# Spreading a slot's small TensorE jobs over the quarters of the next chunk, in a two-layer decoder step

## The reference

```python
# layer 0
z = rms_norm(h, pre_g) @ w_in              # 2048 x 6144: u, pool gate, q, k, v, attention gate
pool_out = pool_linear(window_means(u) - u) * pool_scale      # windows 2, 4, 8, 16
q, k = partial_rope(q), partial_rope(k)    # 8 heads, two 64-wide maps each
o = (softmax(q1 k1) - lam * softmax(q2 k2)) @ v               # causal; sample rows read a paged cache
mix = [pool_out * silu(pool_gate), rms_norm(o) * 0.8 * silu(attn_gate)]
h = h + rms_norm(mix @ w_out, post_g)
# layer 1
z = rms_norm(h, pre_g) @ w_in              # 2048 x 6160: q, k, v, gate, low rank
g = log_sigmoid(lr @ wa2 + ba) / 16
o, state = gla_scan(q, k, v, g, state)     # 4 heads, gated linear attention, causal
h = h + rms_norm((rms_norm(o) * silu(gate)) @ w_out, post_g)
```

## Time and profile before

| | |
|---|---|
| runs | 2369.33, 2361.41, 2366.83 us; median 2366.83 |
| span of the profiled execution | 2367.4 us, and no time of its own beside it |
| TensorE, DVE, ACT, POOL busy | 91%, 35%, 27%, 34% of the span |
| mean granted TensorE clock | 0.924 of 2.4 GHz |
| where the time lies | start to 60 us, four pairs to 1047, output projection to 1248, layer 1's norm to 1307, four heads to about 2133, output projection to 2327, results to the end |

### The profile page before, as it was taken

The page is one execution under the profiler, slowest core; times in us unless marked ns, Lnnn a source line. Parts: engine busy times, 40 slices in busy tenths (PEclk is TensorE's granted clock), DMA queues, the critical chain, the costliest instruction groups (busy, mean ns, idle before and its releaser), DMA issues.

```text
span 2367.4 us, 40345 instructions
## 1 busy us (share of the span) xinstructions
PE 2160.6 (91%) x15341; PEld 1989.5 (84%) x15341; DVE 827.4 (35%) x1391; ACT 646.5 (27%) x1158; POOL 816.3 (34%) x369
## 2 busy tenths in 40 slices
PE   6987998799979997889997999999999999979996
PEld 5986897698869887779995997898799789859995
DVE  4345224522444234550007225305423430642004
ACT  5121212212221212132214324323332332432222
POOL 2242233312241324245546332241232134225554
PEclk8997899879988899789998999999999999989997
DMA  6433333332343234343322354244334424434332
GB/s 209 129 103 90 92 100 86 107 90 75 97 125 93 69 87 116 97 139 97 88 74 97 85 145 143 73 117 134 118 91 132 143 74 124 126 106 145 89 89 73
DMA packets 357441, 252.57 MB, mean 107 GB/s; under 512 B 15135, under 2 KB 324784, under 8 KB 356720
## 3 DMA queue, kind: packets, MB, share of 16 engines
q1 hardware_dynamic: 274892, 148.98, 22.2%
q10 hardware_dynamic: 82372, 101.18, 13.3%
HBM read 213.61 MB, written 36.96 MB: 106 GB/s over the span
## 4 chain that ended last, share of the span: by engine, by line
PE 79%; DVE 8%; issue 5%; ACT 3%; ACTq 2%; POOL 2%; DMA 1%; POOLq 0%; DVEq 0%; SPq 0%
PE proj L972 60%; PE scratch L972 12%; PE score L972 5%; PE scratch L975 2%; ACTq L710 1%; POOL mix L566 1%; DVE sall L1447 1%; DVE probw L1412 1%; DVE ek L1695 1%; POOL mix L581 1%; DVE mix L1443 0%; ACTq L706 0%; DVE small L1411 0%; DVE xlo L1323 0%; DVE qblk L1393 0%
## 5 line engine op out<-in xcount | busy, mean ns | idle before, releaser
L972 PE MATMUL proj<-xhi,wlo 128*128 128x268 f32 x4128 | 1224.7, 297 | 68.3 <-DVE xlo L1323 27.8
L972 PE MATMUL proj<-xlo,whi 128*128 128x268 f32 x4128 | 1209.6, 293 | 0.0
L972 PE MATMUL proj<-xhi,whi 128*128 128x268 f32 x4128 | 1208.4, 293 | 0.0
L512 POOL TENSOR_TENSOR wlo<-wraw,whi 128x1024 fp32r<-128x1024 f32 x258 | 626.8, 2439 | 1069.0 <-ACT whi L592 1069.0
L972 PEld LDWEIGHTS proj<-xhi,wlo 128*128 128x128 f32 x4128 | 808.3, 196 | 92.7 <-issue 71.6
L972 PEld LDWEIGHTS proj<-xlo,whi 128*128 128x128 f32 x4128 | 806.9, 195 | 1.2
L972 PEld LDWEIGHTS proj<-xhi,whi 128*128 128x128 f32 x4128 | 803.3, 195 | 0.0
L592 ACT ACTIVATE whi<-wraw 128x1024 fp32r<-128x1024 f32 x258 | 265.3, 1048 | 612.1 <-PE proj L972 297.8
L1313 DVE TENSOR_TENSOR tz<-proj,rstd 128x536 f32<-128x536 f32 x72 | 51.5, 715 | 393.1 <-PE proj L972 392.6
L533 POOL TENSOR_TENSOR kv<-kv,qb 128x1024 f32<-128x1024 f32 x32 | 76.3, 2383 | 230.6 <-DMA kv<-in_cache_k 153.7
L1605 DVE TENSOR_SCALAR mix<-proj,cols 128x536 f32 x32 | 24.8, 776 | 349.2 <-ACT te L598 177.7
(11 more groups left out here) (252 smaller groups left out, 1915.1 us busy)
## 6 DMA issues: line engine op xcount, KB each, us to landing
wraw<-in_w_in SPq DMA_DIRECT2D x192, 512.0 KB, 3.9
wraw<-in_w_out SPq DMA_DIRECT2D x64, 512.0 KB, 4.0
kv<-in_cache_k ACTq DMA_DIRECT2D x128, 128.0 KB, 2.6
kv<-in_cache_v ACTq DMA_DIRECT2D x128, 128.0 KB, 2.4
sst<-in_state_gla ACTq DMA_DIRECT2D x32, 512.0 KB, 4.7
out<-sst ACTq DMA_DIRECT2D x32, 512.0 KB, 3.3
hbuf<-h_residual ACTq DMA_DIRECT2D x2, 4288.0 KB, 13.7
vb<-v_sample_rows ACTq DMA_DIRECT2D x32, 256.0 KB, 5.6
```

Source lines behind the costliest of these rows:

```text
L512: pool.tensor_tensor(wlo[:, slot, :, 0:width], wraw[:, kc, :, 0:width], whi[:, slot, :, 0:width].bitcast(F32), ALU.subtract).then_inc(s_lo, 1)
L972: return pe.matmul(out, lhsT, rhs, start=start, stop=stop, skip_group_check=True)
```

## The change

TensorE no longer runs all jobs of a slot in a row behind the slot's chunk. `spread(plan, s)` deals a slot's jobs, in their order, to four quarters: job i of n goes to quarter `i * 4 // n`. Quarter 0 stays behind the slot's own chunk; the jobs of quarters 1, 2 and 3 are run within the next slot's chunk, after its first 12, 24 and 36 matmuls (`between`). With one job all stays; of two, the second goes to the half of the next chunk; of three, to 0, 1, 2; of four, to 0, 1, 2, 3; of five, to 0, 0, 1, 2, 3; of six, to 0, 0, 1, 2, 2, 3. The jobs of slot 23 stay in a row. The order of the jobs, their waits and the programs of the other engines are as before.

```diff
+def spread(plan, s):
+
+    ops = plan.get(s, "").split()
+    if s == 23:
+        return [ops, [], [], []]
+    return [[op for i, op in enumerate(ops) if i * 4 // len(ops) == q] for q in range(4)]

-            def chunk(n, par, kc, stage):
+            def chunk(n, par, kc, stage, between=((), (), ()), run=None):
...
                         last = matmul(out, whi[:, slot, k, :], xhi[:, kt, x], start=False, stop=kt == KT - 1)
+                        if (a, k) in ((0, 3), (0, 7), (1, 3)):
+                            for op in between[2 * a + k // 4]:
+                                run(op)
...
                 for s in range(24):
-                    chunk(n0 + s // 2, (s // 2) % 2, s % 2, "in0")
-                    for op in PAIR_PLAN.get(s, "").split():
+                    ops = spread(PAIR_PLAN, s - 1)
+                    chunk(n0 + s // 2, (s // 2) % 2, s % 2, "in0", ops[1:], run)
+                    for op in spread(PAIR_PLAN, s)[0]:
                         run(op)
...
                 for c in range(24):
-                    chunk(n0 + c // 2, (1 + c // 2) % 2, c % 2, "in1")
-                    for op in HEAD_PLAN.get(c, "").split():
+                    ops = spread(HEAD_PLAN, c - 1)
+                    chunk(n0 + c // 2, (1 + c // 2) % 2, c % 2, "in1", ops[1:], run)
+                    for op in spread(HEAD_PLAN, c)[0]:
                         run(op)
```

## The result

The changed kernel took 2438.5 us as the median of four runs (2436.6 to 2442.3), the kernel before, timed beside it, 2365.6 us. The ratio is 1.030, with a 95% interval of 1.027 to 1.033: slower by 73 us where the forecast had 51. The forecast range (2386 to 2445) holds it; the narrower range of the forecast's own mechanism (2400 to 2435) does not, by 3.5 us.

What follows compares the result with a forecast made beforehand. The prediction took TensorE's work plus long chains through ACT, DVE and POOL to bound the kernel; +36 us for four pairs and +15 for four heads made +51 on 2367.4, so 2418 us, range 2386 to 2445.

Steps and rivals of the forecast that it cites:

- rival A: V jobs between quarters of a chunk keep full clock, so the kernel gets faster: 2358 us; chance 0.10.
- rival C: Each new idle time costs clock: two more falls a pair, one a head, 3 us each: 2454 us; chance 0.13.
- Rivals B: Pairs: the query-fetch link before chunk 12 does not bind; a pair costs 2.3 us: 2391 us; chance 0.15.
- D: Waits are taken up in pairs and heads, and the change does nothing measurable: 2367 us; chance 0.04.
- Steps 1 and 2: Pairs: later S2A delays query fetch, POOL and chunk 12 by 3.3 us; with S3A and clock, PT3A by 8.5.
- Step 3: Pairs, slot 14: VT1B ends two quarters later, delaying the chain from ACT's copy to PT0B: +3.1 us.
- Step 4: Pairs, slot 17: half of chunk 18 is done while ST waits, ST ready 0.5 us later: −3.1 us there.
- Step 5: Pairs, V0 to V3: V0 ends 2.3 us later, the stretch behind it shortens by 4.9: −2.6 us at the end.
- Step 6: Heads: waits on ACT's copies add 2.9 and 1.4 us, bank waits give 0.5: +3.8 a head, +15 for four.
- the seams: Cutting rows between projection matmuls costs 0; bounds 0 to 0.05 us a cut, about 30 a pair, 15 a head.

Runs made afterwards that it cites:

- the late slots alone: Only slots 17 to 22 of the pairs spread, against the kernel before: 2356.4 us, ratio 0.994.
- slot 14 alone: Only slot 14 of the pairs (O4A VT0B VT1B) spread, against the kernel before: 2386.1 us, ratio 1.008.
- the pairs alone: Jobs spread in the four pairs only, heads in rows, against the kernel before: 2398.1 us, ratio 1.011.
- slots 8 to 16 alone: Only slots 8 to 16 of the pairs spread, against the kernel before: 2402.6 us, ratio 1.014.
- the heads alone: Jobs spread in the four heads only, pairs in rows, against the kernel before: 2405.1 us, ratio 1.015.
- the query first too: The whole change, with ACT issuing slot 10's two query fetches before exps(2), against the kernel before: 2433.5 us, ratio 1.028.
- without slot 21 too: Only the heads spread, with their slot 21 left in a row, against the kernel before: 2398.1 us, ratio 1.012.

## Why the prediction was right, and where it was not

**Direction and mechanism: right.** The engines that hold TensorE up are those of the text, and what rival A needed did not come: the mean clock fell from 0.924 to 0.918. But the time lies outside the range that this mechanism was given (2400 to 2435); it is inside the whole range because that held part of rival C. Rivals B (no wait on `wlo` in slot 12) and D fell with the first wait list. Spreading as such is not harmful: the late slots alone made the kernel faster. It harms where the last job of a slot starts a chain that was already on TensorE's heels.

**Steps 1 and 2 (+8.5 at PT3A): right in kind, somewhat over.** Measured +7.5 in the mean, of it 2.3 (forecast 3.3) at chunk 12. The link through the query fetch is where it was put, worth 3.1 us at PT3A when slot 10 is put back. What the text did not see is that the link has a twin: with the fetch moved early, DVE's combination becomes late by POOL's block. Neither way round is chunk 12 on time.

**Step 3 (+3.1): right in size, wrong in place.** From PT4A to PT0B it took 39.6 us before and 42.7 after, +3.1; slot 14 alone gave +2.4. But the text had the time as a longer wait before PT0B, 9 us in place of 5.8. That wait fell to 1.3 us in pair 1, and one of 4.08 on `wlo` before chunk 17 stood in its place; in the mean of four pairs the wait before PT0B went from 4.0 to 3.3 and those on `wlo` before chunks 16 and 17 from 1.3 to 3.8. I had left POOL's queue out of the chain behind VT1B, and had taken pair 1 for all: pair 2 of the kernel before has no wait before PT0B.

**Step 4 (ST's wait to 5 us):** 7.0 in the mean, 4.5 to 8.4 by pair. Under the forecast, and of no weight, since step 5 takes its place.

**Step 5 (-2.6 from PT0B to the pair's end): right, a little under.** Before 101.1, after 97.2: -3.9. V0 ran 24.2 us behind ST, 1.2 more than before (2.3 forecast), and V0 to V3's end took 43.2 us in place of 46.9. The forecast had V0's end to V3's end at 41.5 us or more, with every V job at V0's 4.75. It measured 38.3 to 40.8 (40.5 to 43.7 before): V0's price, taken at a low clock, was not that of every V job. V jobs of the kernel after (the last in two pieces):

```profile
496.26 3.63 PE L980 MATMUL scratch<-pds,kv 128*128 128x1 f32 x32
506.80 3.69 PE L980 MATMUL scratch<-pds,kv 128*128 128x1 f32 x32
521.32 3.63 PE L980 MATMUL scratch<-pds,kv 128*128 128x1 f32 x32
532.18 1.84 PE L980 MATMUL scratch<-pds,kv 128*128 128x1 f32 x16
535.05 3.12 PE L980 MATMUL scratch<-pds,kv 128*128 128x1 f32 x16 [1.03 <-DMA kv<-in_cache_v]
```

and of the kernel before, where the first, at 4.91, is the one that the chain of the earlier trace rows has at 4.75:

```profile
478.42 4.91 PE L972 MATMUL scratch<-pds,kv 128*128 128x1 f32 x32
493.44 3.73 PE L972 MATMUL scratch<-pds,kv 128*128 128x1 f32 x32
506.90 5.97 PE L972 MATMUL scratch<-pds,kv 128*128 128x1 f32 x32
522.34 4.69 PE L972 MATMUL scratch<-pds,kv 128*128 128x1 f32 x32
```

It is V0 and V2 that gain. V0 takes 3.63 us at a granted clock of 1.00 in all four pairs, where before it took 3.63, 4.91, 4.82 and 5.26; V2 loses its two long cases of 5.9 us. V1 had 3.73 us at 1.00 in its row in every pair and now takes 3.7 to 4.8, and V3 takes up to 6.0, of which up to 1.2 is a wait for its fetch. So rival A's first half was true of some V jobs, up to 2 us each, and of the stage behind PT0B (126 us at half clock where it had 169), but the waits before PT0B brought as much back (82 us where it had 41): 232 against 233 us in all.

**Per pair +6.1 in place of +9.0,** 24 us in the profile and 30 by the pairs alone, against 36. The terms that were over: 1.0 at PT3A, 0.6 at PT4A, 1.3 in the tail.

**Step 6, the heads (+15): the step that failed.** The idle times were forecast as 3.6 and 1.4 us and measured as 3.64 and 1.42. Priced were only they, 3.8 a head; a head cost 8 to 13, the four of them +37 alone and +43 in the profile. The missing term is the clock: in the pairs I charged 2 us for it at PT3A, in the heads nothing, though the earlier trace rows had a wait followed by half clock. Removing the waits took 25 of 37 us away; by the traces 18 of the 37 are idle time and 10 to 11 the price of 24 us more at half clock, and what is left is busy time that I had taken as 0, the seams below.

Rival C had the right idea, priced at one fall a head and two a pair, 3 us each. In the heads the half clock beside the wait of 3.64 us is 27 us over the four, so at most 3.4 us a head: C's fall, at C's price. The rest of the 41 us more is in the stretch near 184 us, 41 us where the kernel before has 27. In the pairs C was right too, and hidden: between 80 us and PT0B the half clock went up by 41 us, so up to 5 us a pair, and behind PT0B it went down by as much, which is A's effect. That these two cancelled was luck; with slots 8 to 16 alone, where there is nothing to cancel, the pairs had 259 us at half clock, and 218 to 234 in four executions of unchanged pairs.

**The sum was near by offset.** +51 was made of 36 and 15, measured are 30 and 37. The seams were taken as 0, with a bound of 0.05 us a cut and about 30 cuts in a pair and 15 in a head. There are 37 and 24, and in the heads they cost about 0.08 us each (7.5 us over four heads), if all that is left over belongs to them. In the pairs some 4 us of TensorE's 8 us more of busy time are not the clock's, 0.03 us a cut.

## What to carry to other kernels

Before a job is moved behind other TensorE work, follow the chain that its result starts, to the job that waits for it, on every queue it passes; a move pays where TensorE was going to wait anyway (here the last six slots of a pair, 12 us), and costs most of its length where the chain had only tenths of a microsecond to spare (chunk 12 came 2.3 us later for a forecast delay of 3.3). Where a move opens an idle time of a few microseconds on TensorE, price the half clock that may follow it too: in the heads 17 us of waits came with 16 to 18 us of clock. And of an in-order queue, look at its order first: one copy issued ahead of less urgent work (TensorE then waits 0.7 us a head for DVE's `sst`, which the heads alone did not) gave back two thirds of what the spread heads lost.

## What the runs showed of the hardware

Four kernels have a wait of 3.64 to 3.67 us in each head, in the midst of dense projection matmuls (the whole change, with the query first too, and the heads alone, without slot 21 too). At each of these sixteen waits, or just over 1 us behind it, a stretch of 3.4 or 6.8 us at half clock begins; with the wait gone the same window ran at 1.00. At half clock a projection matmul starts every 0.22 us and at full clock every 0.12, so such work takes a little less than twice its time at half clock.

A group of 32 matmuls with one column takes 3.63 us at full clock and 5.97 at a granted clock of 0.58. Where it stands does not settle which: V0 between quarters had 3.63 in every pair of the changed kernel, but V1 had 3.73 in its row in every pair of the kernel before and up to 4.8 between quarters.

And two DVE instructions of 0.42 and 0.62 us took 2.46 and 2.58 beside POOL's of 2.3: the block costs a short instruction four to six times its own time, so that the earliest start for POOL's work is not always the best.
